# A hybrid decoder step on one core: 32-row blocks of the scan's triangular systems inverted in one batch on VectorE, and the stages around them rearranged

## The reference

```python
h = _rms(x, w_norm)
aq, ak, av, az, bq, bk, bv, bz, bb, ba, ga, gb = jnp.split(h @ w_in, ...)
# branch a: differential attention, two softmaxes per head, causal for the prompt, over the cache for the samples
aq, ak = _rope(_rms(aq, a_qn), pos), _rope(_rms(ak, a_kn), pos)
o_a = _rms(_diff_attend(aq, k_all, v_all, ...), a_subln) * (1 - lam_init) * silu(az)
# branch b: gated DeltaNet
qkv = silu(short convolution of 4 taps over bq, bk, bv)
q, k = _l2(bq) * B_DK ** -0.5, _l2(bk);  beta = sigmoid(bb);  g = -exp(a_log) * softplus(ba + dt_bias)
# per chunk (prompt) with gc = cumsum(g):
lmat = strict_lower((k * beta) @ k.T * decay);  amat = lmat + I
u, w = triangular_solve(amat, [v * beta, k * beta * exp(gc)])
v_new = u - w @ S;  o = (q * exp(gc)) @ S + (q @ k.T * decay) @ v_new
S = S * exp(gc[-1]) + (k * exp(gc[-1] - gc)).T @ v_new
# per sample: one recurrent step on a state of 4 x 128 x 128
o_b = _rms(o, b_onorm) * silu(bz)
out = x + (sigmoid(ga) * (o_a @ w_up_a) + sigmoid(gb) * (o_b @ w_up_b)) @ w_out
```

## Time and profile before

| what | value |
|---|---|
| median of 3 runs | 1602.59 us |
| the profiled execution's own time | 1601.74 us |
| its span, first to last instruction | 1600.0 us |
| mean granted clock of TensorE | 0.953 |
| TensorE busy | 1422.1 us, 89% of the span |
| VectorE busy | 796.6 us, 50% |
| GpSimd busy | 357.0 us, 22% |
| ScalarE busy | 297.5 us, 19% |
| bytes moved by the DMA engines | 239.74 MB, 150 GB/s over the span |

### The profile page before, as it was taken

The page is one execution under the profiler, slowest core; times in us unless marked ns, Lnnn a source line. Parts: engine busy times, 40 slices in busy tenths (PEclk is TensorE's granted clock), DMA queues, the critical chain, the costliest instruction groups (busy, mean ns, idle before and its releaser), DMA issues.

```text
span 1600.0 us, 23081 instructions
## 1 busy us (share of the span) xinstructions
PE 1422.1 (89%) x8089; PEld 937.1 (59%) x8089; DVE 796.6 (50%) x1411; ACT 297.5 (19%) x850; POOL 357.0 (22%) x257
## 2 busy tenths in 40 slices
PE   3999999988988988986788988989999958959998
PEld 3444866655555555554466766767677745636443
DVE  4546126676776686554565565765533212263001
ACT  2122123223323323222111111121121100000000
POOL 0123101121222131113424324252321100270000
PEclk9999999999999999997999999999999988889999
DMA  7022214444663763665774766767534048214121
GB/s 246 5 83 93 102 52 137 144 128 133 218 204 111 221 215 122 214 212 182 236 241 135 241 201 180 232 186 218 166 113 120 14 156 272 88 44 131 63 79 54
DMA packets 235442, 239.74 MB, mean 150 GB/s; under 512 B 19217, under 2 KB 182902, under 8 KB 234806
## 3 DMA queue, kind: packets, MB, share of 16 engines
q1 hardware_dynamic: 228558, 214.93, 44.0%
q10 hardware_dynamic: 6768, 23.34, 3.7%
HBM read 206.06 MB, written 32.25 MB: 149 GB/s over the span
## 4 chain that ended last, share of the span: by engine, by line
PE 66%; DVE 11%; issue 9%; POOL 5%; DMA 3%; ACT 3%; SPq 2%; DVEq 0%; ACTq 0%; POOLq 0%
PE ps L1425 20%; PE ps L1539 7%; PE ps L1398 7%; PE ps L1708 7%; PE ps L1659 7%; PE ps L1408 4%; PE ps L1486 3%; DVE tr L1071 3%; PE ps L1454 3%; POOL sa L581 2%; DMA sa<-in_cache_v 2%; PE ps L1520 2%; PE ps L1542 1%; DVE sm L1153 1%; PE ps L1364 1%
## 5 line engine op out<-in xcount | busy, mean ns | idle before, releaser
L1425 PE MATMUL ps<-hT,r 128*128 128x344 f32 x1728 | 582.1, 473 | 0.8 <-ACT gb L717 0.8
L1425 PEld LDWEIGHTS ps<-hT,r 128*128 128x128 f32 x1728 | 316.1, 197 | 154.5 <-issue 44.4
L581 POOL TENSOR_TENSOR sa<-sa 128x512 f32<-128x512 f32 x128 | 174.5, 1374 | 336.2 <-DVE sa L1093 305.1
L1398 PE MATMUL ps<-r,hT 128*128 128x512 f32 x256 | 112.2, 593 | 0.0
L1708 PE MATMUL ps<-r,hT 128*128 128x512 f32 x256 | 110.3, 592 | 0.0
L1093 DVE TENSOR_REDUCE sa<-sa 128x8 f32<-128x512 f32 x128 | 86.9, 679 | 43.3 <-POOL sa L581 43.3
L1091 DVE TENSOR_TENSOR sa<-sa 128x512 f32<-128x512 f32 x128 | 102.6, 801 | 2.8 <-DMA sa<-in_cache_k 2.3
L1659 PE MATMUL ps<-tr,r 128*128 128x344 f32 x192 | 66.2, 492 | 42.0 <-DVE hT L1286 22.1
L1454 PE MATMUL ps<-sa 128*2 128x129 f32 x2048 | 77.9, 274 | 24.7 <-DMA sa<-in_cache_v 24.6
L817 ACT ACTIVATE r<-ps,sm 128x128 f32<-128x128 f32 (+7 forms) x64 | 47.1, 739 | 217.7 <-DVE sm L1154 217.7
L1539 PEld LDWEIGHTS ps<-r 128*128 128x128 f32 x576 | 74.0, 193 | 23.1 <-DVE r L1253 5.4
(11 more groups left out here) (265 smaller groups left out, 1768.5 us busy)
## 6 DMA issues: line engine op xcount, KB each, us to landing
sa<-in_cache_k SPq DMA_DIRECT2D x256, 256.0 KB, 3.0
sa<-in_cache_v SPq DMA_DIRECT2D x256, 256.0 KB, 3.5
r<-in_w_f SPq DMA_DIRECT2D x36, 512.0 KB, 4.8
g_dram<-tr ACTq DMA_DIRECT2D x16, 516.0 KB, 4.0
cv_dram<-tr ACTq DMA_DIRECT2D x12, 512.0 KB, 3.0
sa<-g_dram SPq DMA_DIRECT2D x16, 344.0 KB, 3.3
tr<-cv_dram SPq DMA_DIRECT2D x20, 256.0 KB, 4.5
r<-in_x_prompt SPq DMA_DIRECT2D x8, 512.0 KB, 5.0
```

Source lines behind the costliest of these rows:

```text
L581: nc.gpsimd.tensor_tensor(prod[:, 2 * (gp % 2), :], kring[:, 2 * (gp % 3), :], qB[:, j % 2, :], ALU.mult).then_inc(s["even_mul"], 1)
L1398: ins = nc.tensor.matmul(ps[:, n % 4, :], hT[:, k, t * P:(t + 1) * P], wt[c][:, k, :], start=(k == 0), stop=(k == KD - 1))
L1425: ins = nc.tensor.matmul(ps[:, 4 + i % 2, 0:G3], wf[f % 4][:, k * P:(k + 1) * P], hT[:, k, cg * G3:(cg + 1) * G3], start=(k == 0), stop=(k ...
```

## The change

The prompt's tiles are normed one by one: each has its own semaphore, ScalarE squares a tile, GpSimd adds the constant and takes the power for that tile alone, and the next tile's transposes stand in front of a tile's projection. The samples' products move behind the first eight tiles, SyncE's loads are put in the order of use, and the first pages of the cache are loaded ahead of the projections.

The convolution is done per column group, with one tap on ScalarE straight from PSUM, and with two input buffers. The L2 norms of q and k are taken in the dense stream: 16 groups of four transposes in front of column groups, squared on ScalarE, and tables of the running decay, the key's norm and beta are stored to `tab_dram`.

The scan is split in three stages. In `ORDER_1`, `prep` (6 steps a tile) loads q, k, v and a table broadcast over partitions (768 KB), computes the transposed lower matrix and all other operands, and ScalarE stores six of 256 KB to DRAM. In `ORDER_2`, all 8 x 4 x 4 diagonal blocks of 32x32 are gathered, one to a partition, and inverted there by 31 pairs of VectorE operations (`inv`); the inverses are scattered into `x_dram`, which SyncE has zeroed at the start. In `ORDER_3`, `merge` (10 steps) loads a tile's inverse and does the last two doubling levels (24 products of 128x128 in all, w among them), and `state` (8 steps) does the rest for the tile before.

The 17 features in `ORDER_A` are followed by five in `ORDER_1`, three in `ORDER_2` and eleven in `ORDER_3`, which has all its 33 quarter groups a tile in tiles 0 to 3. From tile 4 on, the same dense stream goes on with up projections (11, 11, 10, 16 and 16 steps), whose weights come through the ring of the dense features, a load of 512 KB for each of 24 units; `ORDER_U` has the 32 quarter groups that are left. The 148 steps of `sa` are split as 72, 20, 8 and 48, the last over tiles 0 to 2. The samples' step lies in tiles 3 to 7, and GpSimd updates their state in two halves behind it, beside the up projections and the output.

Constants and the order of the work:

```diff
+N_A, N_1, N_2 = 17, 5, 3
+SA_A, SA_1, SA_2 = 72, 20, 8
...
+    return weave(("dense", N_A * CG), ("att", AH * ATT_STEPS), ("sa", SA_A))
...
+def phase_1():
+
+    return ["dense"] * 8 + weave(("dense", N_1 * CG - 8), ("prep", NT * PREP), ("sa", SA_1))
+
+
+def phase_2():
+
+    return ["dense"] * 6 + weave(("dense", N_2 * CG - 6), ("inv", BLK), ("sa", SA_2))
+
+
...
+
+    order, gates, sa = [], (NFT - N_A - N_1 - N_2) * CG, 9 * SA_STEPS + 4 - SA_A - SA_1 - SA_2
...
-        part = [("dense", nd), ("solve", SOLVE if t else 0), ("prep", PREP if t < NT else 0), ("sa", na)]
+        dense = gates // 4 if t < 4 else 11 if t < 6 else 10 if t == 6 else 16
+        cached = sa // 3 + (sa % 3 if t == 0 else 0) if t < 3 else 0
+        part = [("dense", dense), ("state", STATE if t else 0), ("merge", MERGE if t < NT else 0), ("sa", cached), ("smp", (0, 0, 0, 1, 3, 3, 3, 3, 0)[t])]
         order += weave(*[x for x in part if x[1]])
```

Start, on ScalarE, GpSimd, VectorE and TensorE:

```diff
+        def token_squares(t):
+            n, src = (NS, x_smp[0:NS, :]) if t == NT else (P, x_all[:, t, :])
+            act.wait_ge(s[f"x_in{t}"], 16)
+            if t:
+                act.wait_ge(s["x_sq"], t)
+            nc.scalar.activation(xsq[0:n], src, ACT.Square, scale=D ** -0.5, accum_out=mean_sq[0:n, t:t + 1]).then_inc(s["x_sq"], 1)
...
+        def token_rstd(t):
+            n = NS if t == NT else P
+            po.wait_ge(s["x_sq"], t + 1)
+            link(nc.gpsimd.tensor_scalar(mean_sq[0:n, t:t + 1], mean_sq[0:n, t:t + 1], EPS, None, ALU.add))
+            nc.gpsimd.tensor_tensor(rstd[0:n, t:t + 1], mean_sq[0:n, t:t + 1], half[0:n, 0:1], ALU.pow).then_inc(s["rstd_ready"], 1)
...
+        def scale_tile(t):
+            n, src = (NS, x_smp[0:NS, :]) if t == NT else (P, x_all[:, t, :])
+            dve.wait_ge(s["rstd_ready"], t + 1)
             if t >= 2:
                 dve.wait_ge(s["xT_ready"], t - 1)
-            nc.vector.tensor_scalar(xn[:, u, :], x_all[:, t, :], rstd[:, t:t + 1], None, ALU.mult).then_inc(s["xn_ready"], 1)
...
+        for t in range(NT + 1):
+            scale_tile(t)
+            if t >= 1:
+                evac_hT(t - 1)
+            if t == 4:
+                constants()
+            if t >= 5:
+                rotate_tile(t - 5)
...
+        transpose_x(0)
         for n in range(2 * NT):
             c, t = n // NT, n % NT
+            if n < NT:
+                transpose_x(n + 1)
+                pe.wait_ge(s["hT_ready"], n + 1)
             if t == 0:
                 pe.wait_ge(s[f"wt_in{c}"], 16)
-                project_samples(c, wt[c], HD)
+            if n == NT:
+                pe.wait_ge(s["hT_ready"], NT + 1)
+            if n in (NT, NT + 1):
```

Convolution and silu in thirds (VectorE), the norm's transposes (TensorE):

```diff
+        def conv(f, cg):
+
+            n, c = f - CONV0, conv_cols(cg)
+            y, u = yb[f % 2][:, c], ub[f % 2]
+            dve.wait_ge(s["f_evac_act"], 3 * n + cg + 1)
+            for k in range(3):
+                ins = nc.vector.scalar_tensor_tensor(y, u[:, c.start + k:c.stop + k], convw[:, n, k:k + 1], y, ALU.mult, ALU.add)
+                if k < 2:
+                    link(ins)
+            ins.then_inc(s["conv_u"], 1)
+
+        def silu(f, cg):
+            c = conv_cols(cg)
+            y = yb[f % 2][:, c]
+            dve.wait_ge(s["th_ready"], 3 * f + cg + 1)
+            nc.vector.scalar_tensor_tensor(y, th[:, c], 1.0, y, ALU.add, ALU.mult).then_inc(s["silu_done"], 1)
...
+                    if extra and kind == "norm":
+                        pe.wait_ge(s["silu_done"], 3 * (f - CONV0))
+                        for t in range(4):
+                            ins = nc.tensor.transpose(ps[:, b, t * P:(t + 1) * P], yb[(f - 1) % 2][:, (4 * hf + t) * P:(4 * hf + t + 1) * P], ident[:])
+                        ins.then_inc(s["ntr_ready"], 1)
```

SyncE: the prepared inputs, the inversion's gather and scatter, the loads of a tile:

```diff
+                sp.dma_start(h3(qkv_in[t % 2][:, c, :]), cv_dram[4 * c:4 * c + 4, :, cols].rearrange("h p n -> p h n")).then_inc(s[f"pin{t % 2}"], 16)
...
+            sp.dma_start(tab_in[t % 2], tab_dram[:, t, :].unsqueeze(0).to_broadcast([P, 3, W])).then_inc(s[f"pin{t % 2}"], 16)
...
+        def load_merge(t):
+            if t >= 3:
+                sp.wait_ge(s["tile_done"], t - 2)
+            for dst, src in ((Xs, of_tile(x_dram, t)), (LTs, of_tile(l_dram, t)), (kbgs, kv_dram[t, 2])):
+                dst = dst[t % 3] if src.shape == (P, W) else h3(dst[t % 3])
+                sp.dma_start(dst, src).then_inc(s[f"min{t % 3}"], 16)
+
+        def load_state(t):
+            if t >= 2:
+                sp.wait_ge(s["tile_done"], t - 1)
+            for dst, i in ((qkTs, 0), (qgTs, 1), (kgs, 3), (vBs, 4)):
+                sp.dma_start(dst[t % 2], kv_dram[t, i]).then_inc(s[f"sin{t % 2}"], 16)
+            sp.dma_start(h3(zbs[t % 2]), z_dram[4:8, :, t * P:(t + 1) * P].rearrange("h p n -> p h n")).then_inc(s[f"sin{t % 2}"], 16)
...
+        for u in range(2):
+            sp.wait_ge(s[f"prep_st{u}"], 96 * NT // 2)
+        sp.wait_ge(s["xz_st"], 16)
+        sp.dma_start(Lb, by_block(l_dram)).then_inc(s["Lb_in"], 16)
+        run(ORDER_2, gens)
+        sp.wait_ge(once("inv_done"), nth("inv_done"))
+        sp.dma_start(by_block(x_dram), Xb).then_inc(s["xb_st"], 16)
+        for u in range(2):
+            sp.wait_ge(s[f"y_st{u}"], 16 * GATE0 // 2)
+        sp.wait_ge(s["xb_st"], 16)
+        load_merge(0)
+        run(ORDER_3, gens)
```

ScalarE's stores of a prepared tile:

```diff
+                        act.wait_ge(per_tile("vB_done"), tiles("vB_done", t + 1))
+                        for src, k in ((kbg, 2), (kg, 3), (vB, 4)):
+                            act.dma_start(kv_dram[t, k], src).then_inc(s[f"prep_st{u}"], 16)
+                        act.wait_ge(per_tile("qkT_done"), tiles("qkT_done", t + 1))
+                        act.dma_start(of_tile(l_dram, t), h3(LT)).then_inc(s[f"prep_st{u}"], 16)
+                        for src, k in ((qkT, 0), (qgT, 1)):
+                            act.dma_start(kv_dram[t, k], src).then_inc(s[f"prep_st{u}"], 16)
```

VectorE's part of a prepared tile, the inversion and the merges:

```diff
+                        link(nc.vector.tensor_tensor(kTn, kT, rk, ALU.mult))
+                        nc.vector.tensor_tensor(kTb, kTn, beta, ALU.mult).then_inc(per_tile("kn_ready"), 1)
+                        nc.vector.tensor_tensor(h3(Dx), h3(gc), bh4(causalT), ALU.add).then_inc(per_tile("Dx_ready"), 1)
...
+                        nc.vector.tensor_tensor(LT, ps[:, 0, :], DT, ALU.mult).then_inc(per_tile("LT_done"), 1)
+                        nc.vector.tensor_tensor(qkT, ps[:, 1, :], DT, ALU.mult).then_inc(per_tile("qkT_done"), 1)
...
+        def inv():
+
+            dve.wait_ge(s["Lb_in"], 16)
+            dve.wait_ge(once("Xb_one"), nth("Xb_one"))
+            for j in range(BLK - 1):
+                n, m = BLK - 1 - j, j + 1
+                o = outer[:, 0:n * m].rearrange("p (i c) -> p i c", i=n)
+                link(nc.vector.tensor_tensor(o, Lb[:, j, j + 1:].unsqueeze(2).to_broadcast([P, n, m]), Xb[:, j, 0:m].unsqueeze(1).to_broadcast([P, n, m]), ALU.mult))
+                rows = Xb[:, j + 1:, 0:m]
+                ins = nc.vector.tensor_tensor(rows, rows, o, ALU.subtract)
...
+                X, Y = Xs[t % 3], Ys[t % 3]
+                for i in range(MERGE):
+                    if i == 0:
+                        dve.wait_ge(s[f"min{t % 3}"], 48 * (t // 3 + 1))
+                        nc.vector.transpose(Y, X).then_inc(per_tile("Y0_ready"), 1)
+                    if i == 1:
+                        dve.wait_ge(per_tile("T1_ready"), tiles("T1_ready", t + 1))
+                        nc.vector.tensor_tensor(h3(T1), h3(ps[:, 0, :]), bh4(lmask[:, 0, :]), ALU.mult).then_inc(per_tile("T1_evac"), 1)
+                    if i == 3:
+                        dve.wait_ge(per_tile("D_ready"), tiles("D_ready", t + 1))
+                        nc.vector.tensor_tensor(X, X, ps[:, 0, :], ALU.subtract)
+                        nc.vector.tensor_tensor(Y, Y, ps[:, 1, :], ALU.subtract).then_inc(per_tile("XY_ready"), 1)
+                    if i == 5:
+                        dve.wait_ge(per_tile("T2_ready"), tiles("T2_ready", t + 1))
+                        nc.vector.tensor_tensor(h3(T1), h3(ps[:, 0, :]), bh4(lmask[:, 1, :]), ALU.mult).then_inc(per_tile("T2_evac"), 1)
+                    if i == 7:
+                        dve.wait_ge(per_tile("DT2_ready"), tiles("DT2_ready", t + 1))
+                        nc.vector.tensor_tensor(Y, Y, ps[:, 1, :], ALU.subtract).then_inc(per_tile("Y_ready"), 1)
+                    yield
```

TensorE: one tile's merges and state, the up projections in the dense stream:

```diff
+                LT, X, Y, kbg = (b[t % 3] for b in (LTs, Xs, Ys, kbgs))
+                for i in range(MERGE):
+                    if i == 0:
+                        pe.wait_ge(s[f"min{t % 3}"], 48 * (t // 3 + 1))
...
+                        mm(LT, X, 0).then_inc(per_tile("T1_ready"), 1)
...
+                    if i == 2:
+                        pe.wait_ge(per_tile("T1_evac"), tiles("T1_evac", t + 1))
+                        mm(Y, T1, 0)
+                        mm(T1, Y, 1).then_inc(per_tile("D_ready"), 1)
...
+                        mm(LT, X, 0).then_inc(per_tile("T2_ready"), 1)
...
```

(58 more changed lines are left out.)

1227 lines of the change are left out of this document (610 added, 617 removed).

## The result

The changed kernel takes 1559.51 us (median of 4, 1555.88 to 1561.68) against 1602.27 for the kernel before: a ratio of 0.9731 (0.971 to 0.9752). It is faster, by a third of the 128 us that were forecast. The profiled execution took 1560.54 us, 86.8 more than the 1473.74 of the sum.

A forecast was written before the change was run, and what follows sets the result against it. TensorE's work and its idle bubbles were taken to set the time. From 1601.74 us, the start's 15, the attention's 60 and the scan through up projections' 53 came off: 1473.74, or 1474.6 as median; range 1389 to 1565.

The forecast's parts named there:

- (b): Attention's stage: the convolution in thirds with two input buffers gives back 25 us of TensorE's idle time, bounds 0 and 42.
- (c): The bubble at 720 to 740 us, after the attention: eight dense quarter groups fill it, -18 us, bounds -10 and -20.
- (f): Attention's stage: cache steps come every 6.1 us where SyncE's queue needs 6.23 for three value pages, +15 us.
- (e): Attention's stage: eight more cache steps, with eight value pages, cost +2 us.
- (d): Attention's stage: 64 norm transposes on TensorE at 0.128 us cost +8 us, with squares on ScalarE behind them.
- (a): Attention's stage: 17 features instead of 20 remove 36 quarter groups of 1.155 us, -41.6 us.
- Stage 2: The inversion's stage: a chain of 65 us, 52 of it covered by TensorE's work, gives 58 us, bounds 45 and 95.
- Stage 3, tiles 0 to 2: Third scan stage with 48 cache steps: the slower of SyncE and TensorE sets each tile, 212 us, bounds 178 and 240.
- Start: Up to the attention's stage: norming tiles singly starts the first projection at about 15 us; gain 15, bounds 8 and 25.
- Stage 1: The `prep` stage: 52.4 MB make the DMA engines its bound instead of TensorE; taken as 166 us.
- slow DMA engines: Rival, chance 0.06: stages 1 and 3 to tile 2 get only 202 GB/s, so the kernel is slower, 1626 us.
- the uncovered inversion: Rival, chance 0.15: gather and scatter take 20 us each, stage 2 takes 95, convolution bubbles stay; 1537 us.

The follow-up runs named there:

- 20 features: The changed kernel with 20 features in the attention's stage and 2 in the first scan stage, instead of 17 and 5: 1587.24 us.
- one tap: The changed kernel with two of the convolution's three taps on VectorE left out: 1536.74 us, the attention's stage 22.4 us shorter.
- fixed pages: The changed kernel with cache pages loaded from fixed addresses instead of by a number from the page table: 1506.83 us, tiles 0 to 2 in 199.9.
- ScalarE's pages: The changed kernel with the third scan stage's value pages loaded from ScalarE's queue instead of SyncE's: 1533.25 us, tiles 0 to 2 in 209.3.
- the spread over four tiles: The changed kernel with the last 48 cache steps over tiles 0 to 3 (12 each) instead of 0 to 2 (16 each): 1537.56 us.

## Why the prediction was wrong

The mechanism was right in outline: the scan was shortened by fewer products, the new bounds were in large part those foreseen (`prep`'s bytes, SyncE's queue, a chain around the inversion), and the output stayed. Of the signs named ahead, the first projection (13.4 us), the full DMA engines and the one wait at the first merge (15.9) came, and SyncE's queue without pauses in tiles 0 and 1, not in tile 2; the granted clock of the attention's stage stayed at 0.96. The size was off by a factor of three, in these steps.

- **(b) in the attention's stage**, "I give back 25", failed. Its reading was right: six waits, 28.4 of the 42 us of idle time, stood behind a whole row's taps, and they are gone. But I counted them as time won and put what would take their place at nothing. The waits for the attention are 36.9 us after and 35.2 before, only shorter and more, and 10.0 us of waits for evacuations on ScalarE came on top. The runs show where part of this comes from: the three features taken out would have covered some 11 us of the attention's waits (26.2 with 20 features), and the thirds still hold softmax steps (25.6 with two taps left out). VectorE is busy 375.18 us in the stage, 336.04 before; at the 0.43 of one tap these 39 us would be some 17 us, an estimate. Which of the small new waits would go without the others stays open.
- **(c)**, the bubble, came in the main: its 13.9 us of idle time are gone from this stretch, and a wait of 9.1 us for the first table stands behind the eight quarter groups, in `prep`'s stage. **(f)**, 15 us for SyncE's queue, did not come: with (e) it was 17 for the eight added steps, and they measure 5.6. Together (b), (c) and (f) were to lower the idle time by 28 us (25 + 18 - 15); it fell by 3.4. **(d)**, 8, was 10.4.
- **(a)**, 36 x 1.155, was right as work, but three features are worth 32.1 us of the stage, not 41.6.
- **Stage 2, "58".** VectorE's 45 us (46.8) and the transfers (7.2 and 6.2 for 5.5, 5.7 for 4.5) were nearly right. The term that was mis-sized is the last tile's products and stores, 4.4 us in the sum, which took 16.5 up to the gather: two steps' pages in SyncE's queue and the stores' landing. So the cover, counted as 52 us, stood against a chain that took 82.4 us and not 65. TensorE idled 21.9 us instead of 13.
- **Stage 3, tiles 0 to 2.** The term was SyncE's, and right as cause: fixed pages, ScalarE's pages and the spread over four tiles each show it. Its size was not: 86, 77 and 61 were 90.1, 76.4 and 69.8, and "the rings carry some over: 212" did not happen: TensorE waited 40 times for value pages, 33 of them in tiles 0 and 1. Tile 2 is not the queue's: TensorE is busy 63.0 us there and waits 6.9.
- **Start, "15".** The first projection began at 13.4 us (15). The gain was 8.4 because VectorE keeps up in work but not in order: its scaling waited 3.8 us a tile for squares that stood on ScalarE behind an evacuation. One queue position gave 6.8 back.
- **Stage 1** held: 168.0 for 166, at 300 GB/s with the engines 0.96 busy, where I had 301. That bytes alone set it is not shown, since without a fifth of them it fell by a tenth. By the Trainium skill (DMA: Bandwidth & Descriptors, Specifications) some 358 GB/s would have made it 146, an estimate; here the measurement decides.

The rivals: TensorE was not the bound, the total was well below that of slow DMA engines, and the uncovered inversion (1537) came nearest, but from a chain of 82 us, with gather and scatter of 7 and 6 us, not 20. The range's upper end, 1565, was said to hold stage 1 at 202 GB/s, but 1474.6 + 93 is 1567.6.
